# VectorE computes each weight block's low part one block later than ScalarE rounds its high part

## The reference

```
def first_block(x, c, ...):                 # two layers
    for l in range(2):
        sh1, sc1, g1, sh2, sc2, g2 = split(c @ mod_w[l] + mod_b[l], 6)
        h = rmsnorm(x, norm1_g[l]) * (1 + sc1) + sh1
        x = x + g1 * mixer(h)               # top-k sparse attention + forgetting attention,
                                            # gated, times w_out
        h = rmsnorm(x, norm2_g[l]) * (1 + sc2) + sh2
        u = causal_conv3(h @ w_up[l])       # 1024 -> 2 * 2816
        a, b = split(u, 2)
        x = x + g2 * ((silu(a) * b) @ w_down[l])
    return rmsnorm(x, final_g)

def second_block(x, mem, ...):              # two layers
    for l in range(2):
        h = rmsnorm(x, norm_pre[l])
        u = h @ w_in[l]                     # feeds five branches of width 256:
        ys = hgrn2, conformer, short_conv, window_attention, memory_attention
        merged = sum(sigmoid(h @ w_gate[l, n]) * (ys[n] @ w_branch[l, n]) for n in range(5))
        x = x + rmsnorm(merged @ w_out[l], norm_post[l])
    return x
```

## Time and profile before

| | |
|---|---|
| time, median of three runs | 1596.11 us (1595.07 to 1596.52) |
| the profiled execution: its own time | 1595.57 us |
| its span | 1593.4 us |
| TensorE busy, share of the span | 1518.2 us, 95% |
| VectorE | 1148.6 us, 72% |
| ScalarE | 828.3 us, 52% |
| mean granted clock of TensorE | 0.981 |

### The profile page before, as it was taken

The page is one execution under the profiler, slowest core; times in us unless marked ns, Lnnn a source line. Parts: engine busy times, 40 slices in busy tenths (PEclk is TensorE's granted clock), DMA queues, the critical chain, the costliest instruction groups (busy, mean ns, idle before and its releaser), DMA issues. The chain is left out here.

```text
span 1593.4 us, 31319 instructions
## 1 busy us (share of the span) xinstructions
PE 1518.2 (95%) x12608; PEld 1450.3 (91%) x12608; DVE 1148.6 (72%) x2186; ACT 828.3 (52%) x1509; POOL 56.5 (4%) x60
## 2 busy tenths in 40 slices
PE   6999999999999988999999899999999799999997
PEld 4888898999988988999999898999999799999997
DVE  5667566888546675669986678877876678878774
ACT  3554445655435544456655554554455554644453
POOL 1000001000010000020002000000000100000000
PEclk9999999999999999999999999999999899999999
DMA  9754454766667432445554532543445343543430
GB/s 393 281 185 188 160 215 183 266 241 249 254 265 292 180 139 80 138 183 210 186 185 181 216 139 104 183 145 147 140 154 210 108 158 108 187 156 133 160 133 27
DMA packets 47407, 289.19 MB, mean 181 GB/s; under 512 B 9944, under 2 KB 11992, under 8 KB 12832
## 3 DMA queue, kind: packets, MB, share of 16 engines
q1 hardware_dynamic: 38880, 280.83, 47.6%
q10 hardware_dynamic: 8384, 6.36, 1.2%
HBM read 284.91 MB, written 2.26 MB: 180 GB/s over the span
## 5 line engine op out<-in xcount | busy, mean ns | idle before, releaser
L1991 DVE TENSOR_TENSOR w_lo<-ring,w_hi 128x1024 fp32r<-128x1024 f32 x436 | 526.6, 1229 | 254.5 <-ACT w_hi L1626 252.7
L1331 PE MATMUL bank<-h_hi,w_hi 128*128 128x256 f32 x2256 | 637.5, 290 | 9.2 <-ACT h_hi L1705 3.7
L1332 PE MATMUL bank<-h_hi,w_lo 128*128 128x256 f32 x2256 | 626.7, 285 | 0.0
L1337 PE MATMUL bank<-h_lo,w_hi 128*128 128x256 f32 x2256 | 579.1, 285 | 0.0
L1626 ACT ACTIVATE w_hi<-ring 128x1024 fp32r<-128x1024 f32 x436 | 448.0, 1053 | 114.1 <-PE bank L1337 113.8
L1331 PEld LDWEIGHTS bank<-h_hi,w_hi 128*128 128x128 f32 x2256 | 437.7, 194 | 24.5 <-issue 18.5
L1332 PEld LDWEIGHTS bank<-h_hi,w_lo 128*128 128x128 f32 x2256 | 438.2, 194 | 0.5 <-issue 0.5
L1337 PEld LDWEIGHTS bank<-h_lo,w_hi 128*128 128x128 f32 x2256 | 409.2, 194 | 0.0
L1331 PE MATMUL bank<-a_hi,w_hi 128*128 128x256 f32 x352 | 99.8, 283 | 0.9 <-DVE w_lo L1991 0.6
L1332 PE MATMUL bank<-a_hi,w_lo 128*128 128x256 f32 x352 | 98.4, 280 | 0.0
L1337 PE MATMUL bank<-a_lo,w_hi 128*128 128x256 f32 x352 | 98.3, 279 | 0.0
(11 more groups left out here) (338 smaller groups left out, 2343.1 us busy)
## 6 DMA issues: line engine op xcount, KB each, us to landing
ring<-weights SPq DMA_DIRECT2D x266, 1024.0 KB, 4.9
pos_bias<-scratch ACTq DMA_DIRECT2D x4, 512.0 KB, 5.8
x<-x_t ACTq DMA_DIRECT2D x1, 1024.0 KB, 6.2
scratch<-line ACTq DMA_DIRECT2D x1, 1024.0 KB, 8.5
mem_x<-mem_t ACTq DMA_DIRECT2D x1, 1024.0 KB, 6.5
out_t<-x SPq DMA_DIRECT2D x2, 512.0 KB, 2.6
co<-const SPq DMA_DIRECT2D x1, 462.0 KB, 6.6
levels_f<-levels ACTq DMA_DIRECT2D x1, 448.0 KB, 14.1
```

The source lines that it names most:

```text
L1331: pe.matmul(to, WH[:, b % SPLIT, o, :], hi[:, k, :], start=(i == 0), stop=False)
L1332: pe.matmul(to, WL[:, b % SPLIT, o, :], hi[:, k, :], start=False, stop=False)
L1337: last = pe.matmul(to, WH[:, b % SPLIT, o, :], lo[:, k, :], start=False, stop=(i == n - 1))
L1991: ve.tensor_tensor(WL[:, b % SPLIT], ring_half(b), WH[:, b % SPLIT].bitcast(F32), ALU.subtract).then_inc(w_lo_v, 1)
```

## The change

A step gets a second bound, `st.behind`, one below `st.upto` once the first norm has been passed, as long as the list of blocks hasn't come to its end. VectorE splits up to `st.behind`; ScalarE still up to `st.upto`. The order of chunks, the loads, the buffers and TensorE's program stay as they are.

```
@@ Step
-        self.kind, self.subs, self.first, self.upto = kind, subs, first, None
+        self.kind, self.subs, self.first, self.upto, self.behind = kind, subs, first, None, None
@@ schedule
         if st.kind == "mod":
             order.append(st.chunk)
+        st.behind = st.upto - 1 if begun and st.upto < len(p.blocks) - 1 else st.upto
         begun = begun or st.kind == "norm"
@@ VectorE's walk over the steps
                 late = st.kind in ("wo1", "dn") and st.j >= KD - 2
                 if late:
                     do[st.kind](st)
-                split_to(st.upto)
+                split_to(st.behind)
                 if st.kind in do and not late:
                     do[st.kind](st)
```

## The result

The changed kernel takes 1579.53 us (median of 4 runs, 1577.07 to 1585.68), the kernel before in the same comparison 1596.32: ratio 0.990, 95% interval 0.987 to 0.993. The profiled execution took 1579.18, 16.4 less than the one before.

The account below looks back on a forecast made before the run. TensorE's work plus its stalls was taken as the bound. Gains of 15.0 us, losses of 13.25 and clock of -3.2 summed to -5.0, so 1591.1 us; the forecast's own range was 1586 to 1596, the whole range 1580 to 1602.

Parts of the forecast that it names:

- the 252.7 us: VectorE's 163 waits for w_hi in the kernel before, its largest idle time; claimed not to be the prize.
- First layer's up projection, 8.4: Loss: subtraction held over the norm comes after up 0, so a mod chunk loads late; TensorE stalls 8.4 us.
- Second layer's, 3.2: Loss at the second layer's up projection: w_lo comes late for up 2; TensorE stalls 3.2 us.
- Down projection, 1.65: Loss in the first layer's down projection: mod chunks later at four groups without slack, 1.65 us in sum.
- rival 4: First layer's down projection: each mod chunk late by a whole subtraction, plus clock spells; 1601.7 us, chance 0.17.
- L2200 and the bias line, 2.3: Gain: TensorE's waits at L2200 (1.3) and the bias line (1.0) both go, 2.3 us.
- probs_t, 10.4: Gain: TensorE's stalls for probs_t in window, forgetting and sparse attention shorten by 10.4 us in sum.
- Rival 1: What is late next, ScalarE's exponentials, takes a quarter of the gains; 1596.6 us, chance 0.12.
- hgrn2 stage, 2.3: Gain: h_val one subtraction (1.15 us) earlier, twice in the kernel, 2.3 us; waits for ScalarE's results stay.
- Clock, -3.2: Half-clock spells behind stalls: 7.0 us back, new stalls bring 2.5 and 1.3; net -3.2, from 0 to -7.0.
- Rival 3: The clock gives nothing back for the shortened stalls; 1598.2 us, chance 0.11.
- Rival 2: The new stalls don't come, as TensorE's two places have slack; 1575.7 us, chance 0.15.

Follow-up runs that it names:

- e3: The kernel before with the change in the hgrn2 stages of the last two layers alone; 1585.42 us, ratio 0.993.
- e1: The changed kernel with the full bound at the two roots before the up projections, so the held-back blocks are subtracted before the norm; 1567.09 us.
- e2: The kernel before with only the two held-back subtractions moved behind up 0 of the up projections; 1611.46 us, ratio 1.009.
- e4: The changed kernel with the full bound at the roots before both up projections and in the first layer's down projection; 1565.03 us.
- e5: The changed kernel with VectorE's full bound, hence its wait for w_hi, put back before hg_exp at 16 steps; 1588.98 us.
- e9: The changed kernel with the full bound at both up-projection roots, the first down projection and the second layer's up 1; 1564.08 us, ratio 0.979.
- e7: The kernel before with the change in the attention stages of the last two layers alone; 1586.77 us, ratio 0.993.
- e11: The changed kernel, unedited, timed again beside the kernel before; 1578.39 us, ratio 0.988.
- e8: The changed kernel with the full bound at both up-projection roots, second layer's up 1 and first down projection, elsewhere VectorE two blocks behind; 1573.60 us.

## Why the prediction was right in direction and short by 11.6 us

- **What bounds the kernel, and that the 252.7 us are no prize**: right. In e3 221.3 of them stand and the time falls by 11.5; in the changed kernel 140 of them went for 16.8.
- **First layer's up projection, 8.4**: 8.33. **Second layer's, 3.2**: 3.14. e1 and e2 show that the two subtractions alone cause them and, with their clock, cost 12.4 to 14.5 us.
- **Down projection, 1.65**: 2.7 by the waits (3.6 to 6.3), 2.1 by time (e4 against e1). Mis-sized by 1 us, inside the bounds of 0 and 7.0; rival 4 falls.
- **L2200 and the bias line, 2.3**: 2.3.
- **probs_t, 10.4**: 11.8 (15.2 with ScalarE's share, to 3.4). Rival 1, which has ScalarE late next, is seen in its mark (ScalarE's share rose from 0.9 to 3.2) but the net gain is above the forecast all the same. It shows once more at 628.2, where the prediction counted the spell as gone: ScalarE's half is 1.42 us late there now, and the spell stays.
- **hgrn2 stage, 2.3**: 4.9. This is the step that failed. "Waits for what ScalarE makes stay, as ScalarE's program is the same" took an unchanged program for unchanged times. ScalarE waited 72.6 us for VectorE's hg_exp. A wait taken from VectorE returned to VectorE through ScalarE: the earlier differences made the rounding earlier, and the rounding was what VectorE waited for. e3 and e5 show it from both sides: alone the stage gave 11.5 us, where the prediction's arithmetic gave 4 to 5.
- **Sum of the stalls, -1.75**: -6.3 in idle time. Of the 4.5 between, 2.6 is the hgrn2 term, 1.4 probs_t, some 1.3 small waits that I had held fixed or left out (h_val at the roots, 11.3 to 10.8, is one), less 0.9 more in the losses.
- **Clock, -3.2**: about -6.6, inside the bound of -7.0. The price was too low: the 18 and 36 matmuls of the earlier trace rows take in those that only overlap the ends of the stretch, and with starts 0.213 us apart the spells cost 1.5 and 3.0, not 1.3 and 2.5. The count of spells was short where it hung on the hgrn2 stage: with the stalls there gone altogether, both spells behind them (6.8 us at 1116.4 and 3.4 at 1454.3) go; I had counted the first, in part, and not the second. All spells behind stalls that changed give back 5.7 net. The other 0.9 is chance, as spells behind stalls that stayed come and go: TensorE waits 1.86 us for h_hi near 260 and again near 700 in both kernels, and has a spell behind the first only in the one, behind the second only in the other. Rival 3 falls. The Trainium skill ("TensorE: Matmul & The Clock Gate", section "What's actually happening") has the clock throttled unless active; the trace agrees that the half clock comes with the new long stall, 10.2 us of it at 269.8, but 6.1 of them ran out while TensorE stood still and cost nothing, so this stall's spell cost 1.8 where 2.5 was forecast.
- **Rest**: 3.4 us of TensorE's busy time outside the spells. The forecast priced a stall at its listed wait, and the matmuls next to it come closer too when it goes (2.3); 2.1 went at places without a listed wait, which it didn't count at all, and 1.0 came back. With the 4.5 of the stalls and the 3.4 of the clock this accounts for the 11.4 us between the forecast of -5.0 and the profiled -16.4, to 0.1.
- **Rival 2** (new stalls don't come) would have given 1575.7, near the measured time, and is wrong in its mechanism: the stalls came to the tenth. A time near a rival's is no evidence for it.

## What to carry to other kernels

When a wait of engine A for engine B is taken away, look whether B in turn waits for A before you hold B's times fixed: in such a ring an earlier step comes back as an earlier release, and the gain is larger than the wait removed next to the stall. And when work is allowed to slip by one place in a list of steps, find the places where the list stands still (here over a norm): there one place is not one block's time but the whole stage, and everything that queues on it, loads above all, pays for it. Slip where the steps are short, keep the old bound at those few places: here 1564.1 us against 1579.5 with a slip everywhere.

## What the runs showed of the hardware

- The kernel before scatters from 1591.9 to 1600.1 us over 13 runs of one comparison, and the granted clock goes with it, 0.983 for the fastest and 0.977 for the slowest. e1 and e9, with two of the long stalls less, stay within 0.8 us, at clocks that differ by 0.001 at most; e4, with nearly the same stalls, spreads over 4.2, so this isn't a rule.
- A stall costs more than its listed wait. At the stalls for probs_t near 968, 979 and 990 (0.84, 1.16 and 1.14 us by the profile of before) TensorE passes 1.00, 1.32 and 1.30 us sooner in the profile of e7, where they are gone.
- TensorE's wait for the ring that ends near 30 us, in the opening stretch where the loads run at over 400 GB/s (418 in the window at 30.9), was 0.9 us in the profile of before, 1.0 in that of the changed kernel and in e7's, and 3.0 to 4.5 in the ten others, e11 among them, which is the changed kernel itself. First the profile of before, then e4's, from 20 to 32 us: a row of the timeline and one of the waits.

```profile
23.55 3.64 PE L1412 MATMUL bank<-ring,c_wide 128*32 128x256 f32 x32
...
PE bank L1412 <- DMA ring<-weights: 0.9, 1, 0.9
```

```profile
23.28 1.93 PE L1414 MATMUL bank<-ring,c_wide 128*32 128x256 f32 x32
...
PE bank L1414 <- DMA ring<-weights: 4.3, 1, 4.3
```

The same 32 matmuls take 3.64 us in the three profiles and 1.93 in the ten, so there TensorE only arrives sooner and waits longer for the chunk. The wait ends at 30.2 to 30.5 in the three and in e5 and e8, and at 31.4 to 31.7 in the other eight. Such a difference lies in the execution; between two traces it is worth up to 1.5 us and not the 3 that the waits suggest. What makes the matmuls slow isn't shown.
